# SBUF laid out anew in a two-layer transformer kernel: stationary operands of the token-form products next to x, other tensors at the upper end

## The reference, cut to what matters

```python
# first block (T = 256 tokens, D = 1024)
h = rmsnorm(x, norm_mix_g)
proj = h @ w_in[l]                      # 1024 x 13320, split in q, k, v, gates of three branches
# ... mLSTM (4 heads), short convolution, stick-breaking attention (16 heads) ...
merged = (jax.nn.sigmoid(g_ml) * (y_ml @ w_ml_proj[l])
          + jax.nn.sigmoid(g_sc) * (y_sc @ w_sc_proj[l])
          + jax.nn.sigmoid(g_sb) * (y_sb @ w_sb_proj[l]))
x = x + merged @ w_out[l]
h2 = rmsnorm(x, norm_mlp_g[l])
x = x + jnp.square(jax.nn.relu(h2 @ w_up[l])) @ w_down[l]          # 1024 x 4096, 4096 x 1024
# second block, after a norm
mix = hybrid_mixer(rms_norm(x, pre_mix_norm[l]), w_in_2, ...)      # RG-LRU, gated linear attention, MoBA
x = x + rms_norm(mix @ w_out_2, post_mix_norm[l])
h = rms_norm(x, pre_ffn_norm[l])
f = (jax.nn.silu(h @ w_ffn_gate) * (h @ w_ffn_up)) @ w_ffn_down    # 1024 x 2816 twice, 2816 x 1024
x = x + rms_norm(f, post_ffn_norm[l])
```

## The kernel before, in words

| tensors | start in bytes | start modulo 64 |
|---|---|---|
| `land`, `whi`, `wlo` | 16512, 41088, 65664 | 0 |
| `xT_hi`, `xT_lo` | 90240, 98432 | 0 |
| `x_tok`, `tok`, `con`, `diag`, `row`, `vecs` | 106624 to 126592 | 0 |
| small tensors of norms, to `lamb` | 126944 to 127264 | mixed |
| `mlqT`, `mlkT`, `ymlT_hi`, `ymlT_lo` | 151904, 160096, 151904, 160096 | 32 |
| `ysbT_hi`, `ysbT_lo` | 184672, 192864 | 32 |
| `w_if_hi` (gate weights, after `rel33` and `w_if`) | 213632 | 0 |
| `yscT_hi`, `yscT_lo` | 201056, 209248 | 32 |
| `aT_hi`, `aT_lo` | 127328, 160096 | 32 |
| `y2T_hi`, `y2T_lo` | 127328, 135520 | 32 |
| `a2T_hi`, `a2T_lo` | 147808, 170336 | 32 |

## Time and profile before

### The profile page before, as it was taken

One profiled execution on the slowest core, in us unless ns is written; L12 is line 12 of the kernel. 1 busy time (PEld: TensorE's weight loads), 2 busy tenths in 40 slices (PEclk: granted clock), 3 DMA queues, 4 the chain that ended last, 5 costly groups with the idle time before them and its releaser, 6 DMA issues.

```text
span 964.4 us, 14152 instructions
## 1 busy us (share of the span) xinstructions
PE 935.6 (97%) x6003; PEld 842.0 (87%) x6003; DVE 579.0 (60%) x610; ACT 469.0 (49%) x520; POOL 38.6 (4%) x75
## 2 busy tenths in 40 slices
PE   5999999999999999999999999998999799999996
PEld 4998998899998888888999988898788699999884
DVE  4554645577787445555556644557975666666552
ACT  6334776862445334344555534446654554444341
POOL 0000111120010000000000000010000000000000
PEclk9999999999999999999999999999999799999999
DMA  8567444443255655555555565528612555556641
GB/s 265 186 234 230 147 161 144 133 150 113 88 175 178 207 184 199 193 175 196 175 175 175 175 218 177 195 77 259 218 67 69 171 176 176 175 176 200 211 135 44
DMA packets 99375, 164.01 MB, mean 170 GB/s; under 512 B 4833, under 2 KB 37316, under 8 KB 99185
## 3 DMA queue, kind: packets, MB, share of 16 engines
q1 hardware_dynamic: 99312, 163.11, 51.9%
HBM read 162.03 MB, written 3.16 MB: 171 GB/s over the span
## 4 chain that ended last, share of the span: by engine, by line
PE 93%; DVE 2%; DMA 2%; ACT 2%; issue 1%; SPq 1%; POOL 0%; DVEq 0%; ACTq 0%; POOLq 0%
PE acc L508 14%; PE acc L500 14%; PE acc L510 14%; PE acc L512 14%; PE acc L502 14%; PE acc L501 14%; DMA land<-in_w_in 2%; PE m L527 1%; PE m L574 1%; PE m L563 1%; PE m L552 1%; DVE wlo L1210 0%; ACT lw L988 0%; DVE x_tok L1486 0%; PE m L636 0%
## 5 line engine op out<-in xcount | busy, mean ns | idle before, releaser
L1210 DVE TENSOR_TENSOR wlo<-land,whi 128x2048 fp32r<-128x2048 f32 (+2 forms) x153 | 337.1, 2206 | 242.1 <-ACT whi L865 240.4
L865 ACT ACTIVATE whi<-land 128x2048 fp32r<-128x2048 f32 (+2 forms) x153 | 281.7, 1846 | 233.4 <-PE acc L502 164.5
L508 PE MATMUL acc<-xT_hi,whi 128*128 128x256 f32 x1168 | 335.3, 287 | 2.1 <-DVE xT_lo L1247 1.8
L510 PE MATMUL acc<-xT_lo,whi 128*128 128x256 f32 x1168 | 332.2, 284 | 0.0
L512 PE MATMUL acc<-xT_hi,wlo 128*128 128x256 f32 x1168 | 332.1, 284 | 0.0
L508 PEld LDWEIGHTS acc<-xT_hi,whi 128*128 128x128 f32 x1168 | 225.8, 193 | 6.8 <-issue 4.2
L510 PEld LDWEIGHTS acc<-xT_lo,whi 128*128 128x128 f32 x1168 | 225.9, 193 | 0.1
L512 PEld LDWEIGHTS acc<-xT_hi,wlo 128*128 128x128 f32 x1168 | 225.8, 193 | 0.0
L500 PE MATMUL acc<-whi,xT_hi 128*128 128x512 f32 (+2 forms) x240 | 91.9, 383 | 0.0
L502 PE MATMUL acc<-whi,xT_lo 128*128 128x512 f32 (+2 forms) x240 | 90.5, 377 | 0.0
L501 PE MATMUL acc<-wlo,xT_hi 128*128 128x512 f32 (+2 forms) x240 | 90.3, 376 | 0.0
(11 more groups left out here) (337 smaller groups left out, 1077.7 us busy)
## 6 DMA issues: line engine op xcount, KB each, us to landing
land<-in_w_in SPq DMA_DIRECT2D x56, 1024.0 KB, 5.1
land<-in_w_up SPq DMA_DIRECT2D x16, 1024.0 KB, 5.3
land<-in_w_down SPq DMA_DIRECT2D x16, 1024.0 KB, 5.1
land<-in_w_ffn_gate SPq DMA_DIRECT2D x22, 512.0 KB, 4.1
land<-in_w_ffn_up SPq DMA_DIRECT2D x22, 512.0 KB, 5.3
land<-in_w_ffn_down SPq DMA_DIRECT2D x10, 1024.0 KB, 5.2
land<-in_w_out SPq DMA_DIRECT2D x6, 1024.0 KB, 5.1
land<-in_w_in SPq DMA_DIRECT2D x12, 512.0 KB, 4.5
```

What stands on the lines that cost most here:

```text
L508: mm(to, whi[:, s, k, cs], xh[:, k0 + k, :], start=first and c % 2 == 0, stop=False, skip_group_check=True)
L510: mm(to, whi[:, s, k, cs], xl[:, k0 + k, :], start=False, stop=False, skip_group_check=True)
L865: activate(whi[:, u % PARTS, 0:m, 0:w], land[:, u % LANDS, 0:m, 0:w], ACT.Copy).then_inc(hi_ready, 1)
L1210: v.tensor_tensor(wlo[:, u % PARTS, 0:m, 0:w], land[:, u % LANDS, 0:m, 0:w], whi[:, u % PARTS, 0:m, 0:w].bitcast(F32), ALU.subtract).then_ ...
```

## The change

The program is the same, instruction for instruction; only the places of the tensors in SBUF change.

- The reserved area at address 0 shrinks from 16 KiB to 1 KiB.
- `whi`, `wlo`, `xT_hi`, `xT_lo` come first at the lower end. Behind them come the tensors of the branches, with `ymlT`, `ysbT` and `yscT` early; `aT` starts at the same place in its stage, and `y2T` and `a2T` right behind `gain_b`, over each other.
- `x_tok`, `tok`, `con`, `diag`, `row`, `vecs`, the small tensors of the norms, `land` and `lamb` are placed from the upper end of SBUF downwards.

From the new list the starts work out as: `whi` 1152, `wlo` 25728, `xT_hi` 50304, `xT_lo` 58496, `ymlT` 66688 and 74880, `ysbT` 83072 and 91264, `yscT` 99456 and 107648, `aT` 66688 and 99456, `y2T` 70784 and 78976, `a2T` 70784 and 93312. All of these are multiples of 64. The tensors at the upper end begin at 229344 downwards: `x_tok` 221152, `tok` 212960, `con` 211424 (each 32 modulo 64), and `land` near 184000.

```diff
-    def sb(name, shape, dt=F32, stack=None):
-        return (stack or ctx).enter_context(nc.sbuf_tensor(name, shape, dt))
+    def sb(name, shape, dt=F32, stack=None, side="left"):
+        return (stack or ctx).enter_context(nc.sbuf_tensor(name, shape, dt, side=side))
-    land = sb("land", [P, LANDS, UK, NG])
     whi = sb("whi", [P, PARTS, UK, NG], F32R)
     wlo = sb("wlo", [P, PARTS, UK, NG], F32R)
     xT_hi = sb("xT_hi", [P, KD, T], F32R)
     xT_lo = sb("xT_lo", [P, KD, T], F32R)
-    x_tok = sb("x_tok", [P, TT, D])
-    tok = sb("tok", [P, TT, D])
-    con = sb("con", [P, K_END])
-    diag = sb("diag", [P, TT, P])
+    x_tok = sb("x_tok", [P, TT, D], side="right")
+    tok = sb("tok", [P, TT, D], side="right")
+    con = sb("con", [P, K_END], side="right")
+    diag = sb("diag", [P, TT, P], side="right")
...
+    land = sb("land", [P, LANDS, UK, NG], side="right")
...
-    sbqT = sb("sbqT", [P, KD, T], stack=area)
-    sbkT = sb("sbkT", [P, KD, T], stack=area)
-    sbv = sb("sbv", [P, TT, D], stack=area)
-    area.close()
-    cT = sb("cT", [P, KD, T], stack=mix)
-    zT = sb("zT", [P, KD, T + CONV_K - 1], stack=mix)
-    conv = sb("conv", [P, 4, T], stack=mix)
     mlqT = sb("mlqT", [P, KD, T], stack=area)
     mlkT = sb("mlkT", [P, KD, T], stack=area)
-    mlv = sb("mlv", [P, TT, D], stack=area)
     area.close()
     ymlT_hi = sb("ymlT_hi", [P, KD, T], F32R, stack=mix)
     ymlT_lo = sb("ymlT_lo", [P, KD, T], F32R, stack=mix)
-    gate = sb("gate", [P, TT, NG], stack=mix)
-    gated = sb("gated", [P, TT, NG], stack=mix)
-    mlo = sb("mlo", [P, TT, D], stack=mix)
     ysbT_hi = sb("ysbT_hi", [P, KD, T], F32R, stack=mix)
...
     yscT_lo = sb("yscT_lo", [P, KD, T], F32R, stack=mix)
+    mlv = sb("mlv", [P, TT, D], stack=area)
+    area.close()
+    gate = sb("gate", [P, TT, NG], stack=mix)
+    gated = sb("gated", [P, TT, NG], stack=mix)
+    sbqT = sb("sbqT", [P, KD, T], stack=area)
...
+    mlo = sb("mlo", [P, TT, D], stack=mix)
...
-    y2T_hi = sb("y2T_hi", [P, KD, T], F32R, stack=two)
-    y2T_lo = sb("y2T_lo", [P, KD, T], F32R, stack=two)
     gain_b = sb("gain_b", [P, D], stack=two)
     a2T_hi = sb("a2T_hi", [P, KF2, T], F32R, stack=area)
     a2T_lo = sb("a2T_lo", [P, KF2, T], F32R, stack=area)
...
     area.close()
+    y2T_hi = sb("y2T_hi", [P, KD, T], F32R, stack=two)
+    y2T_lo = sb("y2T_lo", [P, KD, T], F32R, stack=two)
...
-    nc = bacc.Bacc("TRN2", target_bir_lowering=False, num_devices=1)
+    nc = bacc.Bacc("TRN2", target_bir_lowering=False, num_devices=1, dynamic_dma_scratch_size=1024)
```

More of the change, by code:

```diff
@@ L184, in build @@
     xT_lo = sb("xT_lo", [P, KD, T], F32R)
-    x_tok = sb("x_tok", [P, TT, D])
-    tok = sb("tok", [P, TT, D])
-    con = sb("con", [P, K_END])
-    diag = sb("diag", [P, TT, P])
-    rows = diag[:, 0, :]
[L190 to L198, removed]
+    LC = LRU_W // P
+    x_tok = sb("x_tok", [P, TT, D], side="right")
+    tok = sb("tok", [P, TT, D], side="right")
+    con = sb("con", [P, K_END], side="right")
+    diag = sb("diag", [P, TT, P], side="right")
+    rows = diag[:, 0, :]
+    row = sb("row", [P, T], side="right")
+    vecs = sb("vecs", [P, V_ROWS], side="right")
+    squares = sb("squares", [P, 7, 2, TT], side="right")
+    mean_sq = sb("mean_sq", [P, 7, TT], side="right")
+    rstd = sb("rstd", [P, 7, TT], side="right")
+    factor3 = sb("factor3", [P, TT], side="right")
+    mhalf = sb("mhalf", [P, 1], side="right")
+    land = sb("land", [P, LANDS, UK, NG], side="right")
+    lamb = sb("lamb", [P, 8, LC], side="right")
     ident = con[:, K_ID:K_ID + P]
@@ L203, in build @@
     mix, area = ExitStack(), ExitStack()
-    sbqT = sb("sbqT", [P, KD, T], stack=area)
-    sbkT = sb("sbkT", [P, KD, T], stack=area)
-    sbv = sb("sbv", [P, TT, D], stack=area)
-    area.close()
-    cT = sb("cT", [P, KD, T], stack=mix)
-    zT = sb("zT", [P, KD, T + CONV_K - 1], stack=mix)
-    conv = sb("conv", [P, 4, T], stack=mix)
-    sb("pad0", [P, KD * T - KD * (CONV_K - 1) - 4 * T], stack=mix)
     mlqT = sb("mlqT", [P, KD, T], stack=area)
     mlkT = sb("mlkT", [P, KD, T], stack=area)
-    mlv = sb("mlv", [P, TT, D], stack=area)
     area.close()
@@ L244, in build @@
     yscT_lo = sb("yscT_lo", [P, KD, T], F32R, stack=mix)
+    mlv = sb("mlv", [P, TT, D], stack=area)
[3 more added lines that the diff above has]
+    sbqT = sb("sbqT", [P, KD, T], stack=area)
+    sbkT = sb("sbkT", [P, KD, T], stack=area)
+    sbv = sb("sbv", [P, TT, D], stack=area)
+    area.close()
+    cT = sb("cT", [P, KD, T], stack=mix)
+    zT = sb("zT", [P, KD, T + CONV_K - 1], stack=mix)
+    conv = sb("conv", [P, 4, T], stack=mix)
+    sb("pad0", [P, KD * T - KD * (CONV_K - 1) - 4 * T], stack=mix)
+    mlo = sb("mlo", [P, TT, D], stack=mix)
     sbw = sb("sbw", [P, 2, 3 * P], stack=mix)
```

## The result

The median of the changed kernel is 959.25 us (four runs, 958.35 to 960.85), beside 964.79 us for the kernel before in the same set; the ratio is 0.9947, interval 0.9932 to 0.9962. The forecast was 957.4 us, in a range of 954.5 to 960.2. The profiled execution has a span of 956.4 us, 8.0 us less than before, and its own time is 958.35 us, the lowest of the four.

A forecast was written before the change was run, and what follows sets the result against it. TensorE was taken as the bound, 93% of the chain, through its matmul cadence. Span 964.43 - 7.0 (operand places) - 0.4 (clock) = 957.0, plus 0.35 to the median: 957.4 us, range 954.5 to 960.2.

The forecast's parts named there:

- The gain: Token-form matmuls with stationary operands other than `xT`: 1128 save 6.67 ns each, 7.52 us, less 0.56, taken as 7.0.
- Height: Reading of the slower token-form matmuls: stationary tiles above a border between 106624 and 127328 cost 6.67 ns more.
- A start at 32 modulo 64: Other reading of the slower token-form matmuls: the stationary tile's start remainder costs the 6.67 ns; slightly favoured.
- The rival of the distance: Excess comes from stationary-to-moving tile distance in KiB, so `aT` stays mostly slow: 964.8, at best 963; chance 0.05.
- The interruptions: Behind 14 insertions of small products or transposes among slower operands, 0.04 us of gain is lost each: 0.56 us.
- The clock: TensorE's two clock dips in the work may shift: up to 5 us back or 1.7 lost; credit taken 0.4 us.
- From the span to the median: Step from the profiled execution's span to the median time: 0.35 us added, 957.0 to 957.4.
- Lower addresses: Rival: all matmuls with `xT`, `whi`, `wlo` lose another 6.67 ns, 28.2 us, giving 929; chance 0.05.
- VectorE's split: Rival: the split slows in its new places, costing 9 to 10 us in the second block's mixer, 967; chance 0.04.
- the blocks of `aT_lo` above the old border: Height-alone rival: 5 to 25 blocks stay slow, 0.13 to 0.67 us, 957.5 to 958.4; chance 0.86 shared with forecast.
- No change: Documentation's 16-byte SBUF cachelines make starts at 32 and 64 equal, so time stays 964.8; no-change outcome chance 0.05.
- The 215.8 ns: Documented back-to-back gap, N / 2.4 + 2.5 ns for 512 columns wherever the operand lies; set against traced 226.7 and 233.3.

The follow-up runs named there:

- kernel 1: Kernel before plus a 32-byte filler behind `lamb`, so the slower operands stay high but start at a multiple of 64; 959.33 us, ratio 0.9944.
- kernel 2: Changed kernel plus a 32-byte filler behind `xT_lo`, so branch and hidden-layer operands stay low at distance 32; 966.18 us, ratio 1.0013.
- kernel 5: Changed kernel with `whi` and `wlo` 32 bytes further and activations at distances 32 (`xT`, `aT`, `y2T`), 48, 64 and 144; 962.48 us, one run.
- 4: Changed kernel with activations at different distances: `aT` 4, `ymlT` 16, `ysbT` 48, `yscT` 72, `a2T` 312; 963.86 us, one run.
- 6: Changed kernel with larger distances: `yscT` and `y2T` 0, `aT` 20, `ysbT` 64, `a2T` 80, `ymlT` 384; 964.84 us, one run.
- 10: Changed kernel with `xT` moved to distance 16 from the weights, all other activations at 0; 949.3 us, ratio 0.9842.
- 12: Changed kernel with `xT` moved to distance 32 from the weights, all other activations at 0; 954.61 us, ratio 0.9877.
- kernel 3: Kernel before with only the reserved area cut to 1 KiB, every tensor 15 KiB lower; 965.58 us, ratio 1.0.
- kernel 7: Changed kernel with 384 bytes ahead of `whi`, operands at multiples of 512, all distances still 0; 963.57 us, one run.
- 11: Changed kernel with `xT` moved to distance 256 from the weights, all other activations at 0; 959.74 us, ratio 0.9947.
- 8: Changed kernel with weight rows and slots spread so each block of a unit has another distance, in 16-byte steps; 965.6 us, one run.
- 9: Changed kernel with weight rows spread so block distances step by 64 bytes, with 16 more for each slot; 964.11 us, one run.

## Why the prediction was right, and where its reading was not

**The gain.** The term was 7.52 less 0.56 us; the four stretches gave 2.44 + 2.48 + 0.22 + 1.73 = 6.87. The cadence of 226.7 and the count of 1128 held.

**The cause.** The sum left two causes open, and both were wrong as put. Height fell with experiments 1 and 2. "A start at 32 modulo 64" describes what these layouts had in common, but 5, 4 and 6 refute it as the rule: the distance between the stationary and the moving tile, modulo 256 bytes, sets the cadence, alone at 0 and together with how a stretch begins at 16 and 32. The change helped since all its activations came to lie at distance 0 from the weights. The forecast was right because the two readings and the distance agree about this one layout. As to the cause that is luck; asked about kernel 5, it would have been wrong.

| distance modulo 256 | token form, 512 columns | feature form, 256 columns |
|---|---|---|
| 0 | 226.7 | 120.0 |
| 16 | 226.7 (4), 226.7 and 233.3 (10) | 116.7, 113.3 and 118.6 |
| 4, 80, 128 | 232.2, 232.2, 232.4 | not shown alone |
| 20, 32, 48, 56, 64, 72, 144, 224 | 233.3 | 116.7 and 117.8 at 32 |

**The rival of the distance** had been given 0.05 and measured in KiB. The evidence held against it was the gate products, whose `w_if_hi` lies 120 KiB from `xT_hi` and showed no excess. That row was no evidence: 213632 - 90240 = 123392 is a multiple of 256, so this pair stood at distance 0. After the change it stands at 112032 - 50304 = 61728, 32 modulo 256, and its cadence went from 113.5 to 117.0 ns; in kernels 10 and 12, at 16 and 0, it settles at 113.3. In kernel 2 it stands at 64 with 118.9, in 4 and 5 at 96 with 117.0, in 6 at 160 with 116.7. Note the sign: these products with 64 stationary columns get slower off distance 0, the feature form with 128 gets faster. But here the weights lie ahead of `xT`, so that 32 is 224 by the tables' definition; no kernel has the two at the same distance other than 0, and the number of columns is not shown to be what turns the sign. I have no rule for it, only these values.

**The interruptions**: without a discount for them the gain would have been 7.52 us; with it 6.96, and 6.87 was measured. Of the 0.42 us that are missing in the `y2T` groups (0.64 at the full cadence, 0.22 measured), the ten places counted there give 0.40.

**The clock.** The credit was 0.4 us; this execution won 1.2 net, out of three parts of other sizes: +1.62 at the start, which I had not thought of, -1.67 in the mixer, the new dip that I had named as possible, and +1.26 at the second dip. It isn't a property of the new layout: kernel 3, with the old one 15 KiB lower, reached the upper level before its first product as well, and its clock fell for 6.8 us each at 665 and 761, like the changed kernel's; kernel 7, with the new one, had the late start of before. Single executions of the kernel before lie up to 3.5 us from their median (962.11 to 967.95 over 23 runs). That the credit had the right sign is luck.

**From the span to the median.** I added 0.35 us, the distance of the median of three to the profiled span before; the profiled execution's own time was not among the numbers. In the changed kernel time less span of the same execution was 958.35 - 956.4 = 2.0, and it is 1.7 to 2.3 in all 23 executions of the kernel before. This is the term that was mis-sized, by 1.6 us. The span was forecast at 957.0 and came at 956.4, 0.6 less, and the median of the four lies 0.9 above the profiled execution: -0.6 + 1.6 + 0.9 = 1.9, the distance between forecast and median. The two misses of span and term went opposite ways. The three runs of before that agreed to 0.02 us were taken as proof of little noise; 23 runs on another chip spread over 5.8 us.

**The other rivals.** Lower addresses are not faster by themselves: the feature form stayed at 120.0. VectorE's split did not slow down, and no wait appeared behind it. That the blocks of `aT_lo` above the old border stay slow is refuted by 226.6 ns over the whole of `aT`. No change, by which a start at any multiple of 16 bytes is as good as another: kernel 1 differs from the kernel before by 32 bytes alone, and `aT` went from 233.3 to 226.8 ns.

**Two reads at once.** The Trainium skill, page "TensorE: Matmul & The Clock Gate", section "Step-by-step: what each phase is for", says that the engine has two independent read ports in SBUF, so that loading the next tile's weights takes no bandwidth from the running matmul. The rows agree with an overlap (weight loads are busy 88% of the span beside matmuls at 97%), but the cadences don't agree with two reads that leave each other alone: with the same instructions, a distance of 16 bytes instead of 256 takes 10.4 us off (10 against 11). The measurement decides. The 215.8 ns in the prediction are, in the section "Back-to-back issue gap" of the same page of the Trainium skill, the gap of a single matmul by itself, which the prediction does not say; no run here came below 226.7. Whether the two reads meet in some part of SBUF is only a guess from this; no run here looked inside.

**Open.** Why the distance counts, why its sign differs between forms, what in the beginning of a stretch chooses among the cadences at 16 and 32 bytes, and the steady values at most distances in the feature form. All tiles of a tensor lie multiples of 256 bytes apart (except in 8 and 9), so it is open too whether a matmul's own weight load counts or the next one's, which runs beside it. Kernels 8 and 9 were meant to map the values and could not, because blocks of a few matmuls don't settle.

## What to carry to other kernels

Where TensorE is the bound, divide the time from first to last start of a steady stretch by the number of matmuls, for each pair of operands; a difference of 3% between equal shapes is not noise, and no busy share shows it. Then look at the starts of the two tiles relative to each other, modulo 256 bytes: a small tensor earlier in the list can shift everything behind it, and one filler of 16 or 32 bytes is worth as much as a new layout. Try several distances, each over a stretch of hundreds of matmuls and for each form by itself, since the best distance of the token form (0) was the worst seen in the feature form. Off distance 0 measure every stretch by itself: behind an interruption it may run at another cadence.

A row that speaks against a rival must be checked for the rival's own variable: it may stand, by chance, just where both readings say the same.

## What the runs showed of the hardware

- Three-pass fp32r matmuls at the full clock, each with its own weight load, never reached the 213.3 ns of 512 columns at 2.4 GHz: 226.7 is the best seen, with 232.2 to 233.3 at most other distances. With 256 columns 120.0, 118.6, 117.8, 116.7 and 113.3 were seen, for 106.7.
- The distance between stationary and moving tile, modulo 256 bytes, decides which of these values occur; at 16 and 32 more than one does, constant within a stretch and chosen anew behind an interruption (10, 12). Common shifts of both (kernel 7, or 5 beside 12), height (1) and multiples of 256 (1, 11) change nothing.
- Without DMAs issued by GpSimd, a reserve for descriptors of 1 KiB instead of 16 has no effect on the time (3: ratio 1.0, 0.9986 to 1.0014).
- Runs of one program spread over some 5.8 us in 965; in the profiles the clock differs at the start and behind the idle spells in the second block.
